# Token rows for the experts: turned by VectorE instead of TensorE, from the third pass on

## The chip, the cores and the metric

One core of one Trainium2 chip runs the whole program. The metric is the device time of one launch in microseconds, median of the runs; lower is better. All numbers are float32.

## The reference, cut to what matters

The model runs 512 tokens of 1024 features through two layers of a first block and then one layer of a second block. The change touches only the mixture of experts, which each of the two layers of the first block has. There each token picks one of 4 groups of experts and in it 2 of 8 experts, so 1024 pairs of token and expert are spread over 32 experts:

```python
g_sel = jnp.argmax(g_logits, axis=-1)
top_p, top_i = lax.top_k(e_prob, TOP_K)          # TOP_K = 2, in the token's group
expert_id = (g_sel[:, None] * EXPERTS_PER_GROUP + top_i).reshape(-1)
...
hid = jax.nn.silu(xb @ w_gate[e]) * (xb @ w_up[e])   # xb: the expert's tokens, 1024 features
return hid @ w_down[e]                               # hidden width 256
...
ys = ys * slot_gate[:, None].astype(ys.dtype)
out = jax.ops.segment_sum(ys, slot_tok, num_segments=N + 1)[:N]
```

## The kernel before

Only the expert part matters here; it runs once in layer 0 (about 484 to 775 us of the profiled execution) and once in layer 1 (about 1328 to 1618 us). Its work is cut into NSEQ = 24 passes. 16 of them are "main" passes: each takes two experts, 64 lanes (slots for tokens) for each, 128 lanes in all. 8 are "tail" passes for the tokens beyond 64 of an expert. The order is written out: main, tail, main, main, tail, main, and so on, so that each three passes in a row hold two main passes and one tail pass.

**Weights.** A main pass needs 6 units of 1 MB: 4 for gate and up (`experts_gu`), 2 for down (`experts_down`). SP loads them in the order of use into `ring`, which has 6 places. A load is issued when the place's last user, a group of matmuls on TensorE, is done (`load`, L3185; function `experts`). A tail pass takes its weights from `TW`, filled by indirect DMAs from GpSimd (POOL), L3053 and L3062, for rows that exist; where no expert has such tokens the indices lie out of bounds and nothing but tiny descriptors move.

**Token rows.** The normalised tokens lie in DRAM as `h_tokens` (512 rows of 4 KB). For pass q POOL gathers 128 rows by one indirect DMA (`gather`, L3032) into `XG[:, q % 2]`, with a table of row numbers `idx` that VectorE has made from counts; empty lanes are out of bounds. The matmuls need features on partitions, so TensorE turns the rows: `turn_x` (L1011) makes 8 transposes of 128x128 against the identity into PSUM, ScalarE copies them to `XGT[:, q % 2]` (`x_copy`, L2777), and `gate_up` (L1037) reads them as the stationary operand.

**The rest of a pass.** `gate_up(q)`: 32 matmuls into one bank; ScalarE's silu (`gate`, L2783); VectorE's product (`hidden`, L1986); two transposes on TensorE (`turn_hidden`, L1047), copied by VectorE (`turned_hidden`, L1979); `down(q)`: 16 matmuls (L1059); VectorE scales the result by the gates (`rows`, L1997); POOL scatters the rows to `expert_rows` in DRAM (`scatter`, L3039).

**Order.** Each engine's order is written out by hand, with semaphores between them. TensorE in the steady state: `turn_hidden(q-1)`, `turn_x(q+1)`, `gate_up(q)`, `down(q-1)`. VectorE: `turned_hidden(q)`, `hidden(q+1)`, `rows(q)`. POOL: `gather(q+2)`, then the tail's weights where one is due, then `scatter(q-2)`. In layer 1 VectorE and ScalarE also work out two tables of sines and cosines (`trig`, lines from L1562 on and L2847 on) after the passes 8 and 14 of this order. Indirect DMAs go by the queue q0 (software_dynamic), the ring's loads by q1 (hardware_dynamic); both are served by the same 16 DMA engines.

The lines that set a pass's two ends on TensorE and the loads behind it:

```python
pe.wait_ge(w_landed[place], 16 * fill)            # unit(): a unit of weights has landed
...
name, value = used[(place, fill - 1)]             # load(): its place is free again
sp.wait_ge(Q[name], value)
```

## Time and profile before

| | us |
|---|---|
| median of 3 runs | 3021.24 |
| lowest and highest | 3016.02, 3024.18 |
| span of the profiled execution | 3017.0 |
| of it: expert part of layer 0, first transpose to last `down` | 486.8 to 772.6 |
| of it: expert part of layer 1 | 1328.4 to 1617.8 |

The profile is of one execution. Its own time is not reported apart from the span of 3017.0 us, which lies inside the range of the runs and 4.2 us under their median. The page gives each engine's busy time and, in 40 slices, the busy share of the 16 DMA engines. PE is TensorE's matmuls, DVE is VectorE, ACT is ScalarE, POOL is GpSimd, SP issues loads. The expert parts are the slices in which the DMA digit is 9.

### The profile page before, as it was taken

How to read it: one execution, taken by the hardware profiler on the slowest of the kernel's cores; microseconds unless marked ns; L12 is line 12 of the kernel's file. 1: busy time of each engine (PE TensorE's matmuls, PEld its weight loads, DVE VectorE, ACT ScalarE, POOL GpSimd, SP SyncE). 2: the span in 40 equal slices, each digit the busy share in tenths (PEclk: the TensorE clock that was granted, in tenths of full speed). 3: DMA queues.
4: the chain of work that ended last, by engine and by line, in shares of the span. 5: the costliest groups of instructions: out<-in, count | busy, mean ns of one | idle time of the engine just before them, and what ended most of it. 6: DMA issues, size and time to landing. Idle time of an engine off the chain costs nothing.

```text
span 3017.0 us, 31787 instructions
## 1 busy us (share of the span) xinstructions
PE 2943.6 (98%) x12506; PEld 1884.5 (62%) x12506; DVE 1308.3 (43%) x2213; ACT 652.7 (22%) x1083; POOL 820.3 (27%) x625
## 2 busy tenths in 40 slices
PE   9999999999899999999998999999999999999998
PEld 7865464333468754643333688888664445888887
DVE  6733443111546435431225644433563464644442
ACT  2035313111210253231112300002112441300011
POOL 5400022222135000222222145542300102254442
PEclk9999999999999999999999999999999999999999
DMA  5211125999522101249996122222211201222220
GB/s 190 84 70 43 54 79 225 388 387 384 205 84 84 70 29 56 85 171 387 379 377 274 70 84 92 90 93 89 86 75 56 84 29 56 80 88 84 84 98 28
DMA packets 81379, 412.67 MB, mean 137 GB/s; under 512 B 25872, under 2 KB 26256, under 8 KB 34768
## 3 DMA queue, kind: packets, MB, share of 16 engines
q1 hardware_dynamic: 56608, 387.57, 33.7%
q0 software_dynamic: 24624, 23.08, 2.3%
q8 instruction: 99, 1.62, 0.2%
q14 instruction: 48, 0.39, 0.0%
HBM read 513.31 MB, written 31.46 MB: 181 GB/s over the span
## 4 chain that ended last, share of the span: by engine, by line
PE 67%; DVE 5%; ACT 1%; issue 1%; DMA 0%; DVEq 0%; POOL 0%; ACTq 0%
PE PS L1103 33%; PE PS L608 6%; PE PS L1037 5%; PE PS L1276 3%; PE PS L569 3%; PE PS L594 3%; PE PS L1059 3%; PE PS L686 2%; PE PS L840 1%; PE PS L895 1%; PE PS L516 1%; PE PS L1339 1%; PE PS L1011 1%; PE PS L1319 1%; PE PS L781 1%
## 5 line engine op out<-in xcount | busy, mean ns | idle before, releaser
L3086 POOL TENSOR_TENSOR ATT<-ring 128x512 f32<-128x512 f32 (+1 forms) x98 | 128.0, 1306 | 1203.4 <-PE PS L1103 689.8
L1103 PE MATMUL PS<-G,ATT 128*128 128x256 f32 x1360 | 321.6, 379 | 0.0
L1103 PE MATMUL PS<-HT,ring 128*128 128x256 f32 x1392 | 317.8, 379 | 3.8 <-ACT HT L2626 2.1
L1103 PE MATMUL PS<-G,ring 128*128 128x256 f32 x1232 | 291.4, 379 | 0.0
L1103 PEld LDWEIGHTS PS<-HT,ring 128*128 128x128 f32 x1392 | 264.1, 190 | 43.6 <-issue 3.5
L1103 PEld LDWEIGHTS PS<-G,ATT 128*128 128x128 f32 x1360 | 258.4, 190 | 36.4 <-issue 0.9
L608 PE MATMUL PS<-HT,ring 128*128 128x512 f32 x576 | 263.2, 600 | 0.0
L2808 ACT ACTIVATE TMP<-PS 128x256 f32<-128x256 f32 x92 | 35.2, 383 | 1053.2 <-PE PS L1103 935.9
L1103 PEld LDWEIGHTS PS<-G,ring 128*128 128x128 f32 x1232 | 234.1, 190 | 31.8
L1037 PE MATMUL PS<-ring,G 128*64 128x512 f32 x1024 | 226.8, 595 | 0.6 <-ACT G L2777 0.6
L608 PEld LDWEIGHTS PS<-HT,ring 128*128 128x128 f32 x576 | 104.5, 190 | 126.6 <-issue 120.2
L3094 POOL TENSOR_TENSOR ATT<-ring 128x512 f32<-128x512 f32 (+1 forms) x97 | 172.2, 1776 | 7.6
L1986 DVE TENSOR_TENSOR G<-PS,G 128x256 f32<-128x256 f32 x48 | 20.4, 425 | 319.4 <-ACT G L2783 319.1
L2057 DVE TENSOR_TENSOR BIG<-PS,TMP 128x256 f32<-128x256 f32 x100 | 42.4, 424 | 258.2 <-ACT TMP L2808 255.3
L1037 PEld LDWEIGHTS PS<-ring,G 128*64 128x64 f32 x1024 | 70.7, 137 | 134.0 <-issue 133.0
L1103 PE MATMUL PS<-HT,ATT 128*128 128x256 f32 x568 | 134.3, 379 | 0.0
L3088 POOL TENSOR_TENSOR ATT<-ring 128x512 f32<-128x512 f32 (+1 forms) x97 | 130.5, 1345 | 0.0
L3039 POOL DMA_INDIRECT expert_rows<-G,ATT x46 | 46.6, 1012 | 308.4 <-DVE G L1997 307.9
L3091 POOL TENSOR_TENSOR ring<-ATT,ring 128x512 f32<-128x512 f32 (+1 forms) x98 | 127.8, 1304 | 7.7
L1059 PE MATMUL PS<-ring,G 128*64 128x512 f32 x512 | 116.1, 594 | 9.7 <-DVE G L1979 5.9
L2057 DVE TENSOR_TENSOR G<-PS,TMP 128x256 f32<-128x256 f32 x40 | 17.0, 424 | 245.3 <-ACT TMP L2808 242.5
L2057 DVE TENSOR_TENSOR TMP<-PS,TMP 128x256 f32<-128x256 f32 x273 | 115.8, 424 | 10.6 <-PE PS L1103 1.3
(383 smaller groups left out, 4370.0 us busy)
## 6 DMA issues: line engine op xcount, KB each, us to landing
ring<-in_stream SPq DMA_DIRECT2D x163, 1024.0 KB
ring<-in_experts_gu SPq DMA_DIRECT2D x128, 1024.0 KB
ring<-in_experts_down SPq DMA_DIRECT2D x64, 1024.0 KB
G<-expert_rows SPq DMA_DIRECT2D x8, 1024.0 KB, 7.6
h_tokens<-G POOLq DMA_DIRECT2D x2, 2048.0 KB, 7.6
XT<-in_xT SPq DMA_DIRECT2D x1, 1024.0 KB, 8.4
G<-in_pT POOLq DMA_DIRECT2D x2, 512.0 KB, 6.2
out_T<-XT SPq DMA_DIRECT2D x2, 512.0 KB, 3.7
```

Of the source, the lines that this page charges most:

```text
L569: mm = pe.matmul(ps[0:m, :], wv[:, k, c:c + m], rhs[:, k, :], start=k == 0, stop=k == nk - 1)
L594: mm = pe.matmul(ps, w[:, k, c:c + P], rhs[:, k, :], start=k == 0, stop=k == nk - 1)
L608: mm = pe.matmul(units["ps"], w[:, k, c:c + P], rhs[:, k, :], start=k == 0, stop=k == KD - 1)
L1037: mm = pe.matmul(PS[r, 4 + q % 2, :], XGT[:, q % 2, k * P + CAP * side:k * P + CAP * (side + 1)], ws[side][:, kk * 512:(kk + 1) * 512], st ...
L1059: mm = pe.matmul(PS[r, n, :], HIDT[:, q % 2, j * P + CAP * side:j * P + CAP * (side + 1)], ws[side][:, j * D + n * 512:j * D + (n + 1) * 512],
L1103: mm = pe.matmul(product(g, name), x[:, k * P:(k + 1) * P], y[:, k, :], start=first and k == 0 and name in opening, stop=last and k == h - ...
L1276: mm = pe.matmul(ps, w[:, k, m % 2 * P:(m % 2 + 1) * P], HP[:, k, :], start=k == 0, stop=k == KD - 1)
L2057: v.tensor_tensor(out, product(g, x), y, ALU.add).then_inc(Q[name], now.inc(name))
L3086: pool.tensor_tensor(a["S1"], a["A21"], a["A22"], ALU.add)\
L3088: pool.tensor_tensor(a["S3"], a["A11"], a["A21"], ALU.subtract)\
L3091: pool.tensor_tensor(a["S2"], a["S1"], a["A11"], ALU.subtract)\
L3094: pool.tensor_tensor(a["S4"], a["A12"], a["S2"], ALU.subtract)\
```

## The change

From the third pass on (q = 2 to 23, 22 passes in each layer) `turn_x` and `x_copy` are gone. POOL gathers a pass's rows by four indirect DMAs of 128 pieces of 1 KB (`gather_squares`). Piece g brings, for the 32 lanes of block g, the i-th quarter of each row to the 32 partitions of block i, so that one VectorE instruction, which transposes each 32x32 block in place on the partitions (`turned_rows`), puts features on partitions. Feature f then lies on partition f // 8, block f % 8, so the host lays out the rows of the gate and up weights in the same interleaved order; the first two passes keep TensorE's transposes, with a stride of 8. The row numbers of the pieces come from four small matmuls (`quad_tables`) behind the first `gate_up`, and VectorE turns them into a table (`quad_rows`). The order of the other work is kept. The core of the diff:

```diff
@@ -37,6 +37,9 @@
...
 PLE = 256
+SQUARE = 32
+SQUARES = P // SQUARE
+QD = D // SQUARES
@@ -208,6 +211,7 @@
...
     moe[:, 208] = i
+    moe[:, 209] = i // SQUARE
     moe[:, 216:216 + NSEQ] = P * np.arange(NSEQ)[None, :]
@@ -261,6 +265,7 @@
...
         HDR = nc.dram_tensor("h_tokens", (S, D), F32, kind="Internal").ap()
+        HQR = HDR.rearrange("t (i d) -> (t i) d", i=SQUARES)
         YDR = nc.dram_tensor("expert_rows", (2 * S, D), F32, kind="Internal").ap()
@@ -329,7 +334,7 @@
...
                        ("lanes", 2 * TT * P), ("pairs", 2 * TT * 3 * NSEQ), ("tab", 2 * NSEQ), ("idx", 2 * NSEQ),
-                       ("gslot", NSEQ)):
+                       ("gslot", NSEQ), ("quad", SQUARES * NSEQ)):
             RT[_n] = ATT[:, _o:_o + _w]
@@ -351,6 +356,7 @@
...
         LAST_TOKENS = RT["lanes"][:, 0:S]
+        QUAD_LANES = RT["lanes"][:, S:2 * S]
         RX = BIG[:, 0:KD, :]
@@ -359,6 +365,10 @@
...
         HTF = HT[:, :, :].rearrange("p a b -> p (a b)")
+
+        def gathered(L, q):
+
+            return 16 * (L * (1 + SQUARES * (NSEQ // 2 - 1)) + 1 + SQUARES * (q // 2))
@@ -1003,13 +1013,10 @@
...
                     g = f"x_gather{q % 2}"
-                    if q > 1:
-                        pe.wait_ge(Q["x_copied"], at[f"moe{L}"]["x_copied"] + q)
-                    pe.wait_ge(Q[g], now.next(g, 16))
+                    pe.wait_ge(Q[g], gathered(L, q))
                     o = turned_at(q)
                     for k in range(KD):
-                        mm = pe.transpose(PSF[:, o + k * P:o + (k + 1) * P],
-                                          XG[:, q % 2, k * P:(k + 1) * P], IDENT)
+                        mm = pe.transpose(PSF[:, o + k * P:o + (k + 1) * P], XG[:, q % 2, k:D:KD], IDENT)
                     mm.then_inc(Q["x_turned"], now.inc("x_turned"))
@@ -1026,8 +1033,17 @@
...
+                def quad_tables():
+
+                    pe.wait_ge(Q["tab_ready"], now.next("tab_ready"))
+                    for g in range(SQUARES):
+                        mm = pe.matmul(PS[:, 7, g * NSEQ:(g + 1) * NSEQ], QUAD_LANES[:, g * P:(g + 1) * P], RT["tab"][:, 0:NSEQ],
+                                       start=g == 0, stop=True, skip_group_check=True)
+                    mm.then_inc(Q["quads_ready"], now.inc("quads_ready"))
+
                 def gate_up(q):
-                    pe.wait_ge(Q["x_copied"], now.next("x_copied"))
+                    name = "x_copied" if q < 2 else "x_blocks"
+                    pe.wait_ge(Q[name], now.next(name))
                     for half in range(2):
@@ -1064,19 +1080,17 @@
...
-                at[f"moe{L}"] = {"x_turned": now.count("x_turned"), "x_copied": now.count("x_copied")}
+                at[f"moe{L}"] = {"x_turned": now.count("x_turned"), "x_blocks": now.count("x_blocks")}
                 at[f"moe{L}_y"] = now.count("y_ready")
...
                 gate_up(0)
+                quad_tables()
                 gate_up(1)
                 turn_hidden(0)
-                turn_x(2)
                 down(0)
...
                     turn_hidden(q - 1)
-                    if q + 1 < NSEQ:
-                        turn_x(q + 1)
                     gate_up(q)
@@ -1966,6 +1980,11 @@
...
                 v.tensor_copy(r["gslot"], PS[:, 7, 2 * NSEQ:3 * NSEQ]).then_inc(Q["dve_step"], now.inc("dve_step"))
+                v.wait_ge(*now.prev())
+                v.tensor_copy(QUAD_LANES.rearrange("p (g i x) -> p g i x", g=SQUARES, i=SQUARES),
+                              IDENT.rearrange("p (g x) -> p g x", g=SQUARES).unsqueeze(2)
+                              .to_broadcast([P, SQUARES, SQUARES, SQUARE]))\
+                    .then_inc(Q["tab_ready"], now.inc("tab_ready"))
@@ -1977,6 +1996,22 @@
...
                     v.tensor_copy(HIDT[:, q % 2, :], PS[:, 6, 0:256]).then_inc(Q["hidT_ready"], now.inc("hidT_ready"))
+
+                def quad_rows():
+
+                    v.wait_ge(Q["quads_ready"], now.next("quads_ready"))
+                    v.wait_ge(*now.prev())
+                    v.tensor_scalar(r["quad"].bitcast(I32), PS[:, 7, 0:SQUARES * NSEQ], float(SQUARES), MC[:, 209:210],
+                                    ALU.mult, ALU.add)\
+                        .then_inc(Q["quad_rows"], now.inc("quad_rows"))
+
+                def turned_rows(q):
+
+                    v.wait_ge(Q[f"x_gather{q % 2}"], gathered(L, q))
+                    v.wait_ge(*now.prev())
+                    v.transpose(XGT[:, q % 2, :].rearrange("p (j g x) -> p g j x", j=KD, g=SQUARES),
+                                XG[:, q % 2, :].rearrange("p (g x j) -> p g j x", j=KD, g=SQUARES))\
+                        .then_inc(Q["x_blocks"], now.inc("x_blocks"))
@@ -1998,8 +2033,11 @@
...
                 hidden(0)
+                quad_rows()
                 for q in range(NSEQ):
                     turned_hidden(q)
+                    if q + 2 < NSEQ:
+                        turned_rows(q + 2)
                     if q + 1 < NSEQ:
@@ -2788,8 +2826,6 @@
...
                     gate(q)
-                    if q + 2 < NSEQ:
-                        x_copy(q + 2)
                     if L == LAYERS - 1 and q == TRIG_AT[0] + 1:
@@ -3019,7 +3055,7 @@
...
-            idx, widx = RT["idx"].bitcast(U32), RT["widx"].bitcast(U32)
+            idx, quad, widx = (RT[n].bitcast(U32) for n in ("idx", "quad", "widx"))
             IOA = bass.IndirectOffsetOnAxis
@@ -3032,6 +3068,16 @@
...
                                         oob_is_err=False).then_inc(Q[f"x_gather{q % 2}"], 16)
+
+            def gather_squares(q):
+
+                c = column(q)
+                for g in range(SQUARES):
+                    i = g * NSEQ + c
+                    pool.indirect_dma_start(out=XG[:, q % 2, g * QD:(g + 1) * QD], out_offset=None, in_=HQR,
+                                            in_offset=IOA(ap=quad[:, i:i + 1], axis=0),
+                                            bounds_check=SQUARES * S - 1,
+                                            oob_is_err=False).then_inc(Q[f"x_gather{q % 2}"], 16)
@@ -3125,11 +3171,16 @@
...
                 no_rows()
-                x0, y0 = at[f"moe{L}"]["x_turned"], at[f"moe{L}_y"]
+                x0, b0, y0 = at[f"moe{L}"]["x_turned"], at[f"moe{L}"]["x_blocks"], at[f"moe{L}_y"]
                 for q in range(NSEQ + 1):
                     if q + 2 < NSEQ:
-                        pool.wait_ge(Q["x_turned"], x0 + q + 1)
-                        gather(q + 2)
+                        if q == 0:
+                            pool.wait_ge(Q["quad_rows"], now.next("quad_rows"))
+                        if q < 2:
+                            pool.wait_ge(Q["x_turned"], x0 + q + 1)
+                        else:
+                            pool.wait_ge(Q["x_blocks"], b0 + q - 1)
+                        gather_squares(q + 2)
                     if 1 <= q < NSEQ and ORDER[q - 1][0] == "tail" and ORDER[q - 1][1] + 1 < TAILS:
@@ -3272,7 +3323,8 @@
...
     out["stream"] = np.stack(stream + f1 + mix + f2)
-    gu = np.concatenate([a[n].reshape(LAYERS, NE, KD, P, EH) for n in ("w_exp_gate", "w_exp_up")], axis=4)
+    gu = np.concatenate([a[n].reshape(LAYERS, NE, P, KD, EH) for n in ("w_exp_gate", "w_exp_up")], axis=4)
+    gu = gu.transpose(0, 1, 3, 2, 4)
     gu = gu.reshape(LAYERS, NE, 2, KD // 2, P, 2 * EH).transpose(0, 1, 4, 2, 3, 5).reshape(LAYERS, NE, P, 2, UNIT)
```

How the instructions stand, at three places. First TensorE at the start of the expert part of layer 0, before (L1011 is `turn_x`, L1037 `gate_up`, L1047 `turn_hidden`, L1059 `down`):

```order
245 L1011 MATMUL PS<-MATS,G 128x128 x16
246 L1037 MATMUL PS<-ring,G 64x512 x16
247 L1037 MATMUL PS<-BIG,G 64x512 x16
248 L1047 MATMUL PS<-MATS,G 128x128 x2
249 L1011 MATMUL PS<-MATS,G 128x128 x8
250 L1059 MATMUL PS<-ring,G 64x512 x8
251 L1047 MATMUL PS<-MATS,G 128x128 x2
252 L1011 MATMUL PS<-MATS,G 128x128 x8
253 L1037 MATMUL PS<-ring,G 64x512 x16
```

and now (L1019 is `turn_x`, L1053 `gate_up`, L1040 `quad_tables`, L1063 `turn_hidden`, L1075 `down`):

```order
245 L1019 MATMUL PS<-MATS,G 128x128 x16
246 L1053 MATMUL PS<-ring,G 64x512 x16
247 L1040 MATMUL PS<-ATT 128x24 x4
248 L1053 MATMUL PS<-BIG,G 64x512 x16
249 L1063 MATMUL PS<-MATS,G 128x128 x2
250 L1075 MATMUL PS<-ring,G 64x512 x8
251 L1063 MATMUL PS<-MATS,G 128x128 x2
252 L1053 MATMUL PS<-ring,G 64x512 x16
```

The groups of 8 transposes that stood before each `down` and each `gate_up` are gone, and 4 small matmuls stand between the first two `gate_up`.

VectorE at the same place, now (L2021 is `hidden`, L2004 `quad_rows`, L1998 `turned_hidden`, L2012 `turned_rows`, L2032 `rows`):

```order
429 L2021 TENSOR_TENSOR G<-PS,G 128x256
430 L2004 TENSOR_SCALAR ATT<-PS,MC 128x96
431 L1998 COPY G<-PS 128x256
432 L2012 STREAM_TRANSPOSE G<-G 128x4x8x32
433 L2021 TENSOR_TENSOR G<-PS,G 128x256
434 L2032 TENSOR_SCALAR G<-PS,ATT 128x1024
435 L1998 COPY G<-PS 128x256
436 L2012 STREAM_TRANSPOSE G<-G 128x4x8x32
```

The transpose of pass q+2 stands between the copy of the turned hidden rows of pass q and the product `hidden` of pass q+1.

POOL's queue, now (L3068 is `gather`, L3077 `gather_squares`, L3085 `scatter`, L3099 and L3108 the tail's weights):

```order
71 L3077 DMA G<-h_tokens,ATT 128x256 x12
72 L3099 DMA BIG<-in_experts_gu,ATT 128x4096 x2
73 L3085 DMA expert_rows<-G,ATT 1024x1024
74 L3077 DMA G<-h_tokens,ATT 128x256 x4
75 L3085 DMA expert_rows<-G,ATT 1024x1024
76 L3108 DMA BIG<-in_experts_down,ATT 128x2048 x2
```

Where one gather of 128x1024 stood for a pass, four of 128x256 stand now; the scatters and the tail's loads queue behind them in the old order.

## Rows read from the trace of the kernel before

**Rows 1.** The page: the span, each engine's busy time, the DMA share in 40 slices.

```profile
span 3017.0 us, 31787 instructions
...
PE 2943.6 (98%) x12506; PEld 1884.5 (62%) x12506; DVE 1308.3 (43%) x2213; ACT 652.7 (22%) x1083; POOL 820.3 (27%) x625
...
DMA  5211125999522101249996122222211201222220
```

**Rows 2.** Timeline of PE, layer 0, two passes and a late one: start, length, line, count [idle before].

```profile
567.61 7.09 PE L1037 MATMUL PS<-BIG,G 128*64 128x512 f32 x32
...
578.06 0.44 PE L1047 MATMUL PS<-MATS,G 128*128 128x128 f32 x2
578.33 1.04 PE L1011 MATMUL PS<-MATS,G 128*128 128x128 f32 x8
579.30 7.09 PE L1037 MATMUL PS<-ring,G 128*64 128x512 f32 x32
...
598.61 3.65 PE L1059 MATMUL PS<-ring,G 128*64 128x512 f32 x16 [0.53 <-issue]
```

**Rows 3.** Waits of PE in the expert part of layer 0 (484 to 775 us): total, times, longest.

```profile
PE PS L1059 <- DVE G L1979: 1.7, 1, 1.7
PE PS L1059 <- issue: 1.6, 4, 0.5
```

**Rows 4.** Busy time of the engines, granted clock, DMA share and GB/s, 490 to 770 us.

```profile
490.00:770.00 280.00, 276.63 (x1364) 104.17 (x1362) 49.91 (x71) 33.09 (x48) 74.53 (x75) 1.00 0.93 367
```

**Rows 5.** DMA queues in the same stretch: packets, MB, share of 16 engines.

```profile
q1 hardware_dynamic: 12971, 94.38, 83.6%
q0 software_dynamic: 11011, 8.14, 9.2%
```

**Rows 6.** SP's loads of the ring of weights, 577 to 599 us: start, length, count.

```profile
578.17 6.01 SPq L3185 DMA_DIRECT2D ring<-in_experts_gu  x4
586.43 9.06 SPq L3185 DMA_DIRECT2D ring<-in_experts_down  x4
```

**Rows 7.** Groups of VectorE instructions that read and write 1024 elements in SBUF.

```profile
L2133 DVE TENSOR_TENSOR BIG<-BIG,ATT 128x1024 f32<-128x1024 f32 x22 | 45.4, 2064 | 2.3
...
L1544 DVE STREAM_SHUFFLE G<-BIG 128x1024 f32<-128x1024 f32 x12 | 15.9, 1326 | 0.0
```

**Rows 8.** Timeline of POOL, 517 to 536 us.

```profile
521.61 1.01 POOL L3039 DMA_INDIRECT expert_rows<-G,ATT  x1 [9.35 <-DVE G L1997]
...
524.24 1.00 POOL L3062 DMA_INDIRECT BIG<-in_experts_down,ATT  x1 [0.30 <-issue]
```

**Rows 9.** DMA queues, 540 to 541.5 us.

```profile
q1 hardware_dynamic: 88, 0.62, 99.2%
q0 software_dynamic: 87, 0.00, 3.3%
```

**Rows 10.** DMA queues, 522 to 525 us.

```profile
q1 hardware_dynamic: 174, 1.28, 100.8%
```

**Rows 11.** DMA queues, 542.5 to 544 us.

```profile
q1 hardware_dynamic: 25, 0.11, 17.3%
q0 software_dynamic: 298, 0.00, 10.2%
```

**Rows 12.** DMA queues, 512 to 522 us, with the count of small packets.

```profile
DMA packets 917, 4.06 MB, mean 406 GB/s; under 512 B 360, under 2 KB 360, under 8 KB 484
...
q0 software_dynamic: 424, 0.51, 14.2%
```

**Rows 13.** Timeline of VectorE at the first passes, layer 0.

```profile
496.61 0.42 DVE L1986 TENSOR_TENSOR G<-PS,G 128x256 f32<-128x256 f32 x1 [12.91 <-ACT G L2783]
503.36 0.42 DVE L1979 COPY G<-PS 128x256 f32<-128x256 f32 x1 [6.33 <-PE PS L1047]
```

**Rows 14.** Timeline of PE at the third pass, layer 0.

```profile
508.95 3.22 PE L1037 MATMUL PS<-ring,G 128*64 128x512 f32 x14
```

**Rows 15.** Timeline of PE behind the first angle block, layer 1.

```profile
1454.09 3.65 PE L1059 MATMUL PS<-ring,G 128*64 128x512 f32 x16 [1.23 <-DVE G L1979]
```

More of the change, by code:

```diff
@@ L275, in build_program @@
                  "gate_scaled rf_ready sum2_ready x1_sum late_sum rtok_sum rtok_ready xp_ready pool_step unit_done wsum_ready t_ready hidden_ready m1_ready silu_done tile_done toep_landed "
-                 "pl_landed gain_landed x_low x_high x_landed pos_landed pos2_landed lam_exp tails_zeroed rx_zeroed hot_ready hot_taken z_store part_done edge_sq edge_tile xsq_ready xsq_used res_scaled res_sum x_0 x_1 w_0 w_1 w_2 gates_scaled roped").split()
+                 "pl_landed gain_landed x_low x_high x_landed pos_landed pos2_landed lam_exp tails_zeroed rx_zeroed tab_ready quads_ready quad_rows x_blocks hot_ready hot_taken z_store part_done edge_sq edge_tile xsq_ready xsq_used res_scaled res_sum x_0 x_1 w_0 w_1 w_2 gates_scaled roped").split()
         Q = {n: ctx.enter_context(nc.semaphore(n)) for n in names}
```

## The prediction

> **What bounds the kernel now.** I began with the page [rows 1]: TensorE is busy 98% of 3017.0 us, and the DMA digit is 9 in the two expert parts alone. Then the timeline of TensorE [rows 2]: a pass takes 579.30 - 567.61 = 11.69 us with no gap, and `turn_x` holds TensorE for 579.30 - 578.33 = 0.97 us of it. Read alone, that says the whole of `turn_x` can be had: 22 passes x 2 layers x 0.97 = 42.7 us. The waits speak against it [rows 3]: `down` waited four times, 1.6 us in all, for something that is no engine, that is, for its weights. Over 280 us the DMA engines are busy 93% [rows 4], with 83.6% for the ring of weights and 9.2% for the indirect DMAs [rows 5]. So TensorE and the weights are nearly level, and what matters is where in three passes the weights are late.
>
> Three passes use 12 units, in 6 places. After the second main pass's `down` (over at 578.06) SP issues four loads for gate and up and two for `down` [rows 6]; TensorE wants the last two at 598.61 - 0.53 = 598.08, and starts at 598.61 [rows 2]. These six loads filled 20.55 us, and TensorE's own work in that stretch is 20.02 us. Two of the cycle's three `turn_x` lie in the stretch. Without them TensorE would be there 1.94 us sooner and wait for weights that come no sooner. Only the third `turn_x`, behind that `down`, shortens the cycle.
>
> **What is removed.** 22 x 8 transposes and 22 copies on ScalarE per layer. From q = 4 on these are 7 cycles of three passes, less one pass: 7 x 0.97 = 6.8 us per layer gained, 13.6 in both. ScalarE's copies lay beside matmuls and count nothing. The bounds of this term: nothing, and 20.5 us in a layer, if the weights could follow.
>
> **VectorE's transposes**, 22 per layer. No such instruction is in the trace. The nearest row is STREAM_SHUFFLE of 128x1024, which also moves data between partitions: 1.33 us; the dearest plain group of this size is 2.06 us [rows 7]. I take 1.33, with 1.2 to 2.7 as bounds (2.7, twice the shuffle, for a source read with a stride of 8). The instruction stands between `turned_hidden(q)` and `hidden(q+1)`, which wait for a `gate_up` of 6.9 us in between. VectorE is busy 49.91 of 280 us [rows 4]. That hides it in all passes but the first. If the cover goes (the rows land late), it and all of `hidden` behind it stand in TensorE's path.
>
> A rule of the Trainium skill speaks against it: "SBUF — State Buffer", in the note on cachelines of 16 bytes, says that accesses which cross to a new line each time pay a penalty. Each element of this source, 32 bytes apart, does; by it the instruction would be nearer to the upper bound. No row here shows it.
>
> **The gathers.** Four DMA_INDIRECT for one. On POOL each has a pitch of 1.31 us (521.61 to 524.24 for two) [rows 8], so a pass costs POOL 3.9 us more. Its 75 instructions of the stretch [rows 4] become 141, x 1.31 = 185 of 280 us: hidden.
>
> On the DMA engines an indirect DMA is 11011 / 75, about 147 packets, 9 per engine [rows 4, 5]. Where both queues are full they are served one for one: 88 packets of the ring, 87 of q0 in 1.5 us, that is 0.27 us per turn on each engine [rows 9]. The ring alone makes 174 in 3 us [rows 10], the same rate, so empty lanes cost the ring nothing; without a ring q0 runs freely, 298 in 1.5 us [rows 11]. Rows that exist cost bytes: in 10 us 124 packets of 4 KB and 300 small ones took 14.2% of 160 us = 22.7 us; with 9 ns for a small one (3.3% of 24 us / 87 [rows 9]) a row takes (22.7 - 2.7) / 124 = 161 ns [rows 12]. A piece of 1 KB I estimate at 161 / 4 + 9 = 49 ns, so four cost 35 ns more than a row. Some 950 rows of a layer x 35 / 16 engines = 2.1 us, two thirds in the stretch that the loads fill: +1.4 us per layer. The upper bound counts the 6650 further small ones too, x 9 / 16 = 3.7 us, of which 2.5: +3.9 in all; the lower is 0.
>
> The Trainium skill, "DMA: Bandwidth & Descriptors", section on queues, rings and completion order, says that an engine changes queues only after a whole packet of some 9 to 17 descriptors. By that a gather's 9 would go in one turn, and four gathers in four. The trace shows single descriptors taking turns, 88 to 87, with the weights' rate undisturbed; a block of 9 per load would give the same ratio, so this one is not closed, and it is a rival below.
>
> **The start.** The row numbers wait for four matmuls behind `gate_up(0)`: at 8 transposes in 1.04 us [rows 2], 0.5 us. `quad_rows` follows `hidden(0)`, done at 497.03 [rows 13], so the four gathers of pass 2 start at 497.3, the last at 501.2. With the ring full nothing of q0 is served for 3.4 us or more (issued 521.61, none before 525 [rows 8, 10]); with 9 turns of 0.27 and a landing of about 1 it lands near 508.5. VectorE holds `hidden(1)` until then: + 1.33 + 0.42, and `gate_up(2)` begins near 510.6, where before it began at 508.95 [rows 14]. +1.6 us per layer; bounds -1.4 (TensorE decides) and +4.5 (3 us later).
>
> **The angle blocks.** In layer 1 TensorE waited 1.23 us for VectorE behind the first of the two [rows 15]. It comes 0.97 us sooner now and waits as much longer: +1.9 in all; bounds 0 and +5 (if the new transpose falls in it).
>
> **Sum.** Per layer -6.8 + 1.4 + 1.6 = -3.8; two layers -7.6; with the angle blocks -5.7 us. The profiled execution has a span of 3017.0, which becomes 3011.3. It is 4.2 us under the median, and I take the difference over: 3021.24 - 5.7 = 3015.5 us. About 0.3%, 9 us, is what a measurement of this kernel can tell from no change, so this counts as the same.
>
> **Rivals.**
>
> *A. The weights can follow.* For: `down` is late in four of eight cycles only, by 0.5 us at most [rows 3], and 7% of the DMA time is free [rows 4]. Against: the gap lies where no place of the ring is free. The floor is 0.93 x 280 = 260 us, + 3 for pieces, against 280: -17 us per layer at the most, about 2989 with the angle blocks; half of it gives 3004. It decides if the loads of the stretch of 20.55 us end 1 us or more before their use.
>
> *B. The rows come late (slower).* Three passes have 3 scatters, 4 loads for tails and 3 gathers on q0: 10 DMAs, 90 turns per engine, beside 12 loads x 9 = 108 of the ring. Now they are 19 DMAs, 171 turns: 63 more than the ring can pair. They must go in the ring's gap of about 2 us per cycle [rows 11], else q0 is backlogged. The loop for one buffer: transpose 1.3 + four issues 5.2 + a scatter and tail loads on POOL 3.9 + start 3.4 + up to 63 turns x 0.27 = 17 + landing 1 = 32 us, against two passes and what TensorE can still do, 21.5 + 6.9 + 1.6 = 30. From a backlog of some 55 turns on, VectorE waits in each cycle, `hidden` behind it, then TensorE. At 1.5 to 3 us per cycle, 7 cycles and 2 layers: +21 to +42, less the 5.7: 3036 to 3057. The margin is thin, but in a wait the ring stands still and q0 empties at once [rows 11], which holds the price to the lower half: 3036.
>
> *C. The transpose is dear* (2.7 us or more). It costs 1.4 more at the start of each layer and up to 3 in the angle blocks: 3021. It cannot be seen against no change.
>
> *D. Whole gathers take one turn.* The even count [rows 9] allows it too. Pass 2 then lands about 2 us sooner in both layers, and nothing is ever backlogged: 3015.5 - 4 = 3011.5. It is the rule of the Trainium skill, "DMA: Bandwidth & Descriptors", cited above.
>
> **How the numbers follow.** Forecast 0.42, A 0.15, B 0.27, C 0.08, D 0.08. Faster by over 0.3% (under 3012.2): all of A but a little, most of D, a fifth of the forecast: 0.28. Slower by over 0.3% (over 3030.3): B, and a little of the forecast's upper bounds: 0.28. Within: 0.44. The range leaves out the low half of A and the upper end of B: 3000 to 3040. The forecast's own range is 3008 to 3024.
>
> **What the profile would show.** Right: TensorE's passes of 10.7 us where no `down` waits; `down` of the first main pass of a cycle late by about 2 us in each cycle, put to no engine; a cycle of 34 to 34.5 us; about 20500 packets on q0 in the stretch; VectorE's transpose near 1.3 us, mostly with no wait. It is wrong by B if VectorE's transpose waits on the DMA in many passes and `turn_hidden` waits for `hidden`; wrong by A if no `down` is late and a cycle is near 33 us.

## The result, and the profile after

The changed kernel takes 3029.91 us (median of 9 runs, 3026.83 to 3033.59); the kernel before, on the same chip, 3019.98 (9 runs, 3015.08 to 3024.18). The ratio is 1.0034, with a 95% interval of 1.0025 to 1.0043: about 10 us slower. The profiled execution has a span of 3029.5 us against 3017.0. The forecast was 3015.5 us, a small gain, in a range of 3000 to 3040. The prediction held that changes under 0.3% can't be told from none; the interval here is 0.2% wide, so the loss is told clearly.

The page of the changed kernel, beside [rows 1]: the span, the busy time of the engines.

```profile
span 3029.5 us, 31343 instructions
PE 2919.5 (96%) x12170; PEld 1851.6 (61%) x12170; DVE 1397.8 (46%) x2261; ACT 608.1 (20%) x1039; POOL 955.4 (32%) x757
```

The stretch of [rows 4] and its DMA queues, as in [rows 5]: busy PE, PEld, DVE, ACT and POOL with their counts, granted clock, DMA share, GB/s; then packets, MB, share.

```profile
490.00:770.00 280.00, 258.22 (x1174) 85.98 (x1172) 93.02 (x91) 9.42 (x24) 141.04 (x140) 0.99 0.94 366
q1 hardware_dynamic: 12971, 94.44, 84.8%
q0 software_dynamic: 11973, 7.80, 9.0%
```

VectorE's new instruction, the group of layer 0, beside [rows 7]:

```profile
L2012 DVE STREAM_TRANSPOSE G<-G 128x1024 f32<-128x1024 f32 x22 | 44.9, 2042 | 3.9 <-DMA G<-h_tokens,ATT 1.4 <-DVE G L1998 0.5
```

TensorE is 276.63 - 258.22 = 18.4 us less busy over 280 us, as intended. POOL issued 140 indirect DMAs instead of 75, yet q0's packets rose only from 11011 to 11973. VectorE's transpose takes 2.04 us and waited 3.9 us in 22 passes for its rows.

The timeline of TensorE from the third pass on, layer 0, beside [rows 14]: start, length, line, count [idle before <- releaser].

```profile
509.86 7.09 PE L1053 MATMUL PS<-ring,G 128*64 128x512 f32 x32
516.78 4.09 PE L1075 MATMUL PS<-BIG,G 128*64 128x512 f32 x16
526.96 0.69 PE L1063 MATMUL PS<-MATS,G 128*128 128x128 f32 x2 [6.09 <-DVE G L2021]
527.58 9.14 PE L1053 MATMUL PS<-ring,G 128*64 128x512 f32 x32
```

What no step of the prediction had: a pause of 6.09 us, once in the layer. TensorE waited for VectorE's `hidden`, and that for ScalarE's `gate`. ScalarE's row names no engine that it waited for ("remote"):

```profile
504.67 0.38 ACT L2821 ACTIVATE G<-PS 128x256 f32<-128x256 f32 x1 [7.64 <-PE PS L1053]
526.00 0.39 ACT L2821 ACTIVATE G<-PS 128x256 f32<-128x256 f32 x1 [20.95 <-remote]
```

It needs only `gate_up(2)`, whose matmuls end by the records at 509.86 + 7.09 = 516.95. It starts at 526.00, 9 us later. SP's next loads, which TensorE's completions release too, start at the same moment:

```profile
526.00 8.14 SPq L3236 DMA_DIRECT2D ring<-in_experts_down  x4
```

Here and below, "completions" are the semaphore events with which TensorE tells the other engines that a group of matmuls is done. After the idle time the granted clock is down (0.50 in the row below), and `gate_up(3)` takes 9.14 instead of 7.09 us:

```profile
525.00:530.00 5.00, 3.04 (x8) 1.06 (x10) 3.21 (x4) 0.39 (x1) 0.91 (x1) 0.50 1.01 389
```

Layer 1 has it at the same pass, and there the matmuls of `down(1)` themselves stand apart:

```profile
1362.85 1.89 PE L1075 MATMUL PS<-BIG,G 128*64 128x512 f32 x8
1364.98 1.02 PE L1075 MATMUL PS<-BIG,G 128*64 128x512 f32 x3 [0.24 <-issue]
1366.41 2.02 PE L1075 MATMUL PS<-BIG,G 128*64 128x512 f32 x4 [0.41 <-issue]
1369.25 0.59 PE L1075 MATMUL PS<-BIG,G 128*64 128x512 f32 x1 [0.82 <-issue]
1373.17 0.69 PE L1063 MATMUL PS<-MATS,G 128*128 128x128 f32 x2 [3.33 <-DVE G L2021]
```

A late completion that no engine's row explains sends one to the engines that were busy without a break just then. POOL's timeline of layer 0:

```profile
498.76 1.05 POOL L3077 DMA_INDIRECT G<-h_tokens,ATT  x1 [6.85 <-DVE ATT L2004]
...
509.65 1.00 POOL L3077 DMA_INDIRECT G<-h_tokens,ATT  x1 [0.69 <-issue]
...
522.77 1.00 POOL L3077 DMA_INDIRECT G<-h_tokens,ATT  x1 [0.30 <-issue]
529.09 1.02 POOL L3085 DMA_INDIRECT expert_rows<-G,ATT  x1 [5.32 <-DVE G L2032]
```

From 498.76 to 523.77 it issues 19 indirect DMAs at a pitch of 1.31 us, with one gap of 0.69. `gate` starts 2.2 us after the last. VectorE's copy behind `turn_hidden(1)`, at the ninth DMA of the run, is late too: it starts at 511.69, 1.8 us after the matmuls' end by the records (509.93) and 0.9 us after VectorE was free for it.

**Where the time went.** The expert part of a layer falls into pieces by TensorE's timeline: the start (first `turn_x` to the end of `down(0)`); eight stretches, each from the end of a second main pass's `down` (the first: of `down(0)`) to the start of the next `down` of a first main pass, with six ring loads in it; and seven rests, each from the start of that `down` to the end of the next, where the third `turn_x` of the cycle stood. The eighth stretch has no loads to wait for; with the last `down` it is 12.94 + 3.65 us everywhere, and it is in the last column alone. Sums in us, layer 0 / layer 1, one profiled execution each:

| kernel | start | first stretch | stretches 2 to 7 | rests | layer |
|---|---|---|---|---|---|
| before | 21.0 / 21.1 | 19.9 / 19.8 | 121.0 / 121.8 | 107.3 / 110.1 | 285.8 / 289.4 |
| changed | 22.0 / 22.1 | 27.3 / 27.4 | 125.2 / 123.8 | 101.2 / 107.4 | 292.3 / 297.3 |
| one_gather | 22.0 / 22.1 | 20.4 / 20.0 | 122.4 / 121.8 | 101.3 / 107.4 | 282.7 / 287.8 |
| before_pieces | 23.3 / 23.4 | 20.3 / 20.0 | 123.7 / 124.5 | 107.4 / 110.2 | 291.2 / 294.6 |
| empty_run | 25.7 / 24.6 | 19.8 / 19.8 | 121.6 / 122.2 | 107.3 / 110.1 | 291.0 / 293.2 |
| third_only | 21.0 / 21.1 | 20.6 / 20.6 | 123.0 / 123.7 | 101.2 / 107.4 | 282.4 / 289.4 |
| stretch_only | 21.0 / 21.1 | 20.6 / 20.6 | 119.7 / 120.0 | 107.4 / 110.2 | 285.3 / 288.5 |

The changed kernel gained 6.1 us in the rests of layer 0 (2.8 in layer 1), lost 4.2 and 2.1 in the stretches, 1.0 at the start, and 7.4 and 7.6 in the first stretch, which holds the pause. Outside these parts the same instructions take up to 4 us more or less from one execution to the next (between the two expert parts 552.7 to 556.8 us), so a few microseconds of a whole run are not read from one timeline.

### The profile page after: what moved, and what is told of

Read it like the earlier page. It is cut to its first block, busy times and chain, and to the rows that moved or that the text cites. A ratio compares the mean times of both kernels' runs of the same rounds, so it can differ in the third digit from the quotient of the medians.

```text
span 3029.5 us, 31343 instructions
## 1 busy us (share of the span) xinstructions
PE 2919.5 (96%) x12170; PEld 1851.6 (61%) x12170; DVE 1397.8 (46%) x2261; ACT 608.1 (20%) x1039; POOL 955.4 (32%) x757
## 4 chain that ended last, share of the span: by engine, by line
PE 87%; DVE 5%; DMA 4%; another core or an unknown queue 1%; ACT 1%; issue 1%; SPq 0%; POOL 0%; DVEq 0%; ACTq 0%; POOLq 0%
PE PS L1117 37%; PE PS L1053 8%; PE PS L618 8%; PE PS L604 5%; PE PS L1075 4%; PE PS L696 4%; PE PS L579 4%; PE PS L1290 4%; DMA ring<-in_experts_gu 3%; PE PS L850 1%; PE PS L791 1%; PE PS L538 1%; PE PS L905 1%; PE PS L914 1%
## 5 line engine op out<-in xcount | busy, mean ns | idle before, releaser
L2844 ACT ACTIVATE TMP<-PS 128x256 f32<-128x256 f32 x92 | 35.3, 384 | 1056.9 <-PE PS L1117 939.7
L1053 PE MATMUL PS<-ring,G 128*64 128x512 f32 x1024 | 233.3, 605 | 10.4 <-DMA ring<-in_experts_gu 9.9
L3077 POOL DMA_INDIRECT G<-h_tokens,ATT x176 | 177.5, 1009 | 110.9 <-issue 49.3
L1053 PEld LDWEIGHTS PS<-ring,G 128*64 128x64 f32 x1024 | 73.0, 139 | 148.2 <-issue 147.4
L1075 PE MATMUL PS<-ring,G 128*64 128x512 f32 x512 | 117.9, 602 | 27.2 <-issue 19.7
L2821 ACT ACTIVATE G<-PS 128x256 f32<-128x256 f32 x48 | 18.4, 384 | 520.3 <-PE PS L1053 329.4
L2021 DVE TENSOR_TENSOR G<-PS,G 128x256 f32<-128x256 f32 x48 | 20.4, 425 | 222.0 <-ACT G L2821 156.8
```

The source lines that it names most:

```text
L1053: mm = pe.matmul(PS[r, 4 + q % 2, :], XGT[:, q % 2, k * P + CAP * side:k * P + CAP * (side + 1)], ws[side][:, kk * 512:(kk + 1) * 512], st ...
L1075: mm = pe.matmul(PS[r, n, :], HIDT[:, q % 2, j * P + CAP * side:j * P + CAP * (side + 1)], ws[side][:, j * D + n * 512:j * D + (n + 1) * 512],
L3077: pool.indirect_dma_start(out=XG[:, q % 2, g * QD:(g + 1) * QD], out_offset=None, in_=HQR, in_offset=IOA(ap=quad[:, i:i + 1], axis=0), bou ...
```

## The experiments

Theory 1 was that POOL's run of gathers makes the pause; theory 2, that it belongs to TensorE's or VectorE's changed program. Each ratio is to the kernel before, run beside it on the same chip. Of each edit its core is shown; in a diff "..." marks what is left out.

**one_gather**: the piece gathers undone alone (with the counts that the engines wait for).

```diff
-                        gather_squares(q + 2)
+                        gather(q + 2)
```

> From the third pass on, the rows are gathered whole again (one indirect DMA per pass instead of four); VectorE's 32x32 transposes, the row-number matmuls and TensorE's shorter program stay. The rows then stand in the wrong order for the transposes, so the output of the expert part isn't the reference's. Theory 1 (the pause of about 8.5 us of TensorE once per layer, at the third pass, comes from POOL's run of 12 back-to-back piece gathers): the pause is gone in both layers, -17, and the pieces' bytes (about -2 in each layer) too: 3009 to 3013 us. Theory 2 (the pause belongs to TensorE's or VectorE's changed program, whatever POOL does): the pause stays, 3024 to 3028 us.

Measured: 3011.93 us, ratio 0.9972 (0.9960 to 0.9983). No pause: TensorE's changed program and VectorE's transposes don't make it by themselves. The third pass, where the changed kernel waits:

```profile
516.83 3.60 PE L1075 MATMUL PS<-BIG,G 128*64 128x512 f32 x16
520.37 0.44 PE L1063 MATMUL PS<-MATS,G 128*128 128x128 f32 x2
520.73 7.32 PE L1053 MATMUL PS<-ring,G 128*64 128x512 f32 x32
```

The stretches 2 to 7 are 2.8 and 2.0 us shorter than in the changed kernel: the price of the pieces in the flow.

**from_sixth**: passes 2 to 5 keep the old way, on every engine (`FIRST = 6`).

```diff
-                        gather_squares(q + 2)
+                        (gather if q + 2 < FIRST else gather_squares)(q + 2)
...
```

> The change begins at the seventh pass (q = 6) instead of the third: passes 2 to 5 use the old way (one gather, TensorE's turn, ScalarE's copy). Theory 1 (burst of gathers behind the late row numbers makes the pause): no burst at the start of the layer, POOL has caught up by then, so no pause; 3029.9 - 17 + 4 passes whose turn_x is back, of which one or two count (2 to 4 us over both layers): 3014 to 3018 us. Theory 2 (the pause comes at the first passes with the new way, wherever they stand): it moves to passes 6 and 7, 3029 to 3033 us.

Measured: 3019.20 us, 0.9991 (0.9982 to 1.0001). No pause in either layer, at pass 6 neither. The sum for the rest was too hopeful by 1 to 5 us.

**before_pieces**: the kernel before, its gathers from the third pass on in four pieces.

```diff
-                        gather(q + 2)
+                        gather_pieces(q + 2)
```

> The kernel before with one edit: from the third pass on the rows are gathered in four pieces of 1 KB, into the same places, so the result is the same; TensorE still turns them. Theory 1: the burst of piece gathers costs here too, a pause at the third pass or a start later by several us per layer: 3030 us or more. Theory 2: pieces cost their bytes alone, 0 to 4 us per layer: 3021 to 3028, no pause. My prediction's term of 1.4 us per layer would give 3023.

Measured: 3026.31 us, 1.0021 (1.0011 to 1.0030). The pieces alone lose 2.3 and 2.2 us at the start of the layers, and 3.0 and 2.9 in the stretches. The pause is there, one pass earlier, as POOL's run is (482 to 501 us). TensorE's first row and ScalarE's `gate(0)`:

```profile
488.29 7.09 PE L1040 MATMUL PS<-ring,G 128*64 128x512 f32 x32 [0.24 <-ACT G L2784]
...
503.51 0.38 ACT L2790 ACTIVATE G<-PS 128x256 f32<-128x256 f32 x1 [14.15 <-remote]
```

The gate comes 503.51 - 495.38 = 8.1 us late, once more 2 us after POOL's last issue.

**early_rows**: the row numbers from VectorE, ahead of the expert part.

```diff
-                quad_tables()
...
+                    v.tensor_scalar(r["quad"][:, g * NSEQ:(g + 1) * NSEQ].bitcast(I32), r["tab"][:, 0:NSEQ], float(SQUARES),
+                                    float(g), ALU.mult, ALU.add).then_inc(Q["quad_rows"], now.inc("quad_rows"))
```

> The changed kernel with the pieces' row numbers worked out by VectorE from the slot table before the expert part (as 4 x row + g), so the four matmuls behind the first gate_up and the wait for them are gone and pass 2's gathers are issued at about 492 instead of 499 us. Each piece then goes to a lane where it does not belong, so the output of the expert part isn't the reference's; the traffic is the same. If the pause comes from POOL's backlog behind late row numbers, it is gone or under 3 us: 3012 to 3018. If it comes from the pieces or the transposes themselves, it stays: 3026 to 3030.

Measured: 3022.04 us, 1.0006 (0.9996 to 1.0017), between the two guesses. The run starts earlier and is shorter (15 DMAs), and `gate(0)` is 7.7 and 7.3 us late; most of it lies beside `gate_up(1)`, so the start takes 22.7 and 22.4 us, 1.8 and 1.3 more than before. In layer 1 the stretches 2 to 7 take 128.9 us, 5 more than in the changed kernel; no row here says why.

**paced**: POOL waits until the pass's gather before has landed, for the passes 3 and 4.

```diff
+                        if q in (1, 2):
+                            pool.wait_ge(Q[f"x_gather{(q + 1) % 2}"], gathered(L, q + 1))
                         gather_squares(q + 2)
```

> The changed kernel with one edit on POOL: the piece gathers of the fourth and fifth pass (q = 3 and 4) wait for the landing of the gather before them, so that at most four gathers are issued in a row at the start of a layer. If an unbroken run of 8 or more indirect DMAs on POOL is what holds TensorE's completions back (theory 1, after the first four runs), the pause at the third pass is gone or under 2 us: 3012 to 3016 us. If it comes from the rows' bytes, the transposes or the place in the program, it stays: 3027 to 3031.

Measured: 3031.76 us, 1.0037 (1.0022 to 1.0051); the expectation failed, and told more than a hit. Two groups of four pass with little harm, and the third pass has no pause. Then POOL makes up what it lost, 23 DMAs from 518.73 to 548.8 us, and TensorE is disturbed from 532 to 550:

```profile
535.04 8.57 PE L1053 MATMUL PS<-BIG,G 128*64 128x512 f32 x32 [3.12 <-issue]
543.42 1.41 PE L1075 MATMUL PS<-ring,G 128*64 128x512 f32 x4
545.63 0.63 PE L1075 MATMUL PS<-ring,G 128*64 128x512 f32 x1 [0.80 <-issue]
```

**empty_run**: in the kernel before, behind the gather of pass 3 (`EMPTY_RUN = 8`):

```diff
...
+                for i in range(EMPTY_RUN):
+                    pool.indirect_dma_start(out=RT["dump"][:, 16 * i:16 * (i + 1)], out_offset=None, in_=small,
+                                            in_offset=IOA(ap=idx[:, column(2):column(2) + 1], axis=0),
+                                            bounds_check=0, oob_is_err=False).then_inc(Q["dumped"], 16)
```

> The kernel before, with 8 more indirect DMAs on POOL behind the gather of the fourth pass (from about 494.2 to 504.8 us), each a gather of 64-byte rows in which all lanes but at most one are out of bounds; the data go to a scratch tile. Nothing waits for them but POOL's own queue. Theory 1a (issuing alone holds TensorE's completion signals back): TensorE pauses in pass 1 or 2 by 2 to 8 us per layer, 3025 to 3035 us. Theory 1b (it takes rows with bytes, 1 KB pieces, in the run): no pause, 3019 to 3022 us.

Measured: 3028.10 us, 1.0031 (1.0018 to 1.0044): 9 us for 16 DMAs that move next to nothing. TensorE's `turn_x(2)`, which waits for nothing of theirs, then POOL's first and last DMA of the run:

```profile
503.66 0.86 PE L1012 MATMUL PS<-MATS,G 128*128 128x128 f32 x5
504.91 0.33 PE L1012 MATMUL PS<-MATS,G 128*128 128x128 f32 x1 [0.38 <-issue]
505.61 0.32 PE L1012 MATMUL PS<-MATS,G 128*128 128x128 f32 x1 [0.37 <-issue]
506.99 0.27 PE L1012 MATMUL PS<-MATS,G 128*128 128x128 f32 x1 [1.07 <-issue]
...
482.96 1.07 POOL L3033 DMA_INDIRECT G<-h_tokens,ATT  x1 [10.70 <-DVE ATT L1963]
...
503.93 1.00 POOL L3055 DMA_INDIRECT ATT<-h_tokens,ATT  x1 [0.30 <-issue]
```

But the empty DMAs do less than the full ones. `gate_up(0)` ends at 496.59, at the eleventh DMA of the run, and its `gate` is 2.0 us late, not 8.1 as in before_pieces at the eleventh; and it starts in the midst of the run, not behind it:

```profile
498.59 0.38 ACT L2784 ACTIVATE G<-PS 128x256 f32<-128x256 f32 x1 [8.03 <-remote]
```

The copy behind `turn_hidden(0)`, at the sixteenth, is 3.4 us late (507.26, where the matmuls end at 503.82).

**spaced_run**: empty_run with a memset of 0.79 us ahead of each of the 8.

```diff
                 for i in range(EMPTY_RUN):
...
+                    pool.memset(RT["filled"], 0.0).then_inc(Q["filled"], now.inc("filled"))
```

> The kernel before with the 8 empty gathers, each behind a memset of 128x800 (about 0.7 us), so that the issues have a pitch of about 2.1 instead of 1.31 us. If issues back to back are what holds TensorE (a queue that fills faster than it empties), the pause is gone: 3018 to 3022 us. If the number of indirect DMAs counts, or POOL's being without a wait, it stays: 3026 to 3032 us.

Measured: 3019.70 us, 1.0001 (0.9991 to 1.0011). The same 8 DMAs at a pitch of 1.95 us cost nothing, though POOL is without a break for longer (`gate(0)` is still 0.8 us late, hidden beside `gate_up(1)`):

```profile
503.27 1.04 PE L1012 MATMUL PS<-MATS,G 128*128 128x128 f32 x8
504.24 3.65 PE L1060 MATMUL PS<-ring,G 128*64 128x512 f32 x16
...
503.05 1.00 POOL L3058 DMA_INDIRECT ATT<-h_tokens,ATT  x1 [0.16 <-issue]
504.06 0.78 POOL L3057 MEMSET ATT<- 128x800 f32 x1
505.00 1.00 POOL L3058 DMA_INDIRECT ATT<-h_tokens,ATT  x1 [0.16 <-issue]
```

**empty_four**: `EMPTY_RUN = 4`.

> As the kernel before with the empty gathers, but 4 of them instead of 8: POOL's unbroken run from 483 us ends near 500 instead of 505 us. If TensorE's completions are held from about the tenth DMA of an unbroken run until the run ends, the hold is about 5 us shorter, and mostly hidden: pass 2 starts at most 1 us later than in the kernel before, 3019 to 3023 us. If each empty gather costs a fixed sum, half of the 9 us: 3023 to 3025.

Measured: 3019.19 us, 1.0004 (0.9994 to 1.0014); the start is 21.0 us as before. `gate(0)` is 2.0 and 2.2 us late here too, but that lies beside `gate_up(1)`, and the run is over before TensorE needs an answer. Not a price per DMA.

**busy_run**: the loop holds only a memset of 128x900, ten times (9.0 us).

> The kernel before with 10 memsets of 128x900 on POOL in place of the empty gathers, about the same 10 us of unbroken work at the same place, no DMA. If any busy POOL holds TensorE's completions, a pause like that of the empty gathers, 3025 to 3030 us. If it is the issuing of indirect DMAs, nothing: 3018 to 3021 us.

Measured: 3020.28 us, 0.9997 (0.9988 to 1.0007). No `gate` is later than before. A busy POOL as such does no harm.

**spaced_pieces**: back in the changed kernel.

```diff
                 for g in range(SQUARES):
                     i = g * NSEQ + c
+                    if 3 <= q <= 4:
+                        if now.count("filled"):
+                            pool.wait_ge(Q["filled"], now.count("filled"))
+                        pool.memset(RT["filled"], 0.0).then_inc(Q["filled"], now.inc("filled"))
```

> The changed kernel with a memset of 128x700 (0.7 us) on POOL ahead of each piece gather of the fourth and fifth pass, so that these 8 issues have a pitch of about 1.9 instead of 1.31 us. Nothing else moves, and the result is the reference's. If back-to-back issues make the pause, it is gone or under 2 us at the third pass, 3013 to 3018 us; it may return at passes 5 to 7, where POOL makes up the lost time back to back, then 3022 to 3030. If something else of the change makes it, it stays at the third pass, 3030 us.

Measured: 3020.97 us, 0.9995 (0.9985 to 1.0004): 9 us under the change's median (0.39% by the two ratios), by doing more. The third pass:

```profile
517.10 3.60 PE L1075 MATMUL PS<-BIG,G 128*64 128x512 f32 x16
520.63 0.44 PE L1063 MATMUL PS<-MATS,G 128*128 128x128 f32 x2
521.00 7.09 PE L1053 MATMUL PS<-ring,G 128*64 128x512 f32 x32
```

A smaller one stays behind it: `gate(3)` is 3.0 us late, and `gate_up(4)` takes 8.41 us. What else lengthens its layers (289.0 and 292.0 us in the profiled execution) is TensorE's clock, which falls behind two waits for weights in each:

```profile
566.00 5.25 PE L1075 MATMUL PS<-ring,G 128*64 128x512 f32 x16 [2.46 <-issue]
```

The same `down` takes 3.65 us at the full clock; here the granted clock is 0.59 from 566 to 570 us.

**gaps_all**: one memset per group of four, from the fourth pass on.

```diff
+                        if q >= 1:
...
+                            pool.memset(RT["filled"], 0.0).then_inc(Q["filled"], now.inc("filled"))
                         gather_squares(q + 2)
```

> The changed kernel with one memset of 128x700 (0.7 us) on POOL ahead of each pass's four piece gathers, from the fourth pass on; the four are still back to back. If a short gap every 4 to 7 DMAs is enough to break the run, no pause: 3012 to 3016 us. If the mean pitch counts (1.31 becomes about 1.45 us), the pause is only shorter: 3020 to 3028 us.

Measured: 3028.72 us, 1.0026 (1.0015 to 1.0038). The pause moves to the fourth and fifth pass. `gate(3)` is 8.1 and 8.6 us late; in the change `gate(2)` was 9.1 and 9.2. A gap per group is not enough. Over what length of a run the pitch has to be wider isn't tested.

**third_only** (`NEW = range(5, 24, 3)`) and **stretch_only** (`NEW = [q for q in range(6, 24) if q % 3 != 2]`): the new way for the passes in `NEW` alone.

```diff
-                        gather_squares(q + 2)
+                        (gather_squares if q + 2 in NEW else gather)(q + 2)
```

> The new way only for the passes q = 5, 8, ... 23, whose turn_x stands behind the down of the first main pass, outside the stretch that six ring loads fill; all others in the old way, and the row-number matmuls behind turn_hidden(1). The result is the reference's. If my reading of the cycle is right, all of the gain is here: 7 x -0.86 = -6.0 and pieces for 7 of 22 passes, +1, so -5 per layer and about 3010 us, with no pause. If the gain is spread over all passes (or TensorE's work bounds everywhere), a third of it: 3016 or more.

> The opposite choice: the new way only for the passes q >= 6 whose turn_x lies in the stretch of the six ring loads (12 passes per layer), q = 5, 8, ... 23 in the old way. By my reading of the cycle the 12 x 0.97 = 11.6 us per layer that TensorE is spared there are given back whole as waits for weights, and the pieces of 12 passes cost 1 to 2 us: 3021 to 3024 us. If the weights can follow (rival A), it is faster by up to 20 us: 3000 to 3010.

Measured: third_only 3011.96 us, 0.9972 (0.9961 to 0.9984); stretch_only 3017.17 us, 0.9992 (0.9983 to 1.0002). Seven passes per layer give 7 us by the medians; the twelve others, with more of TensorE's time removed, nothing that can be told from none. The profiled execution of third_only shows only half of the 7: 3.4 us in layer 0 and none in layer 1, where the gain of the rests (2.8) goes again in the first stretch (0.8, with the row-number matmuls in it) and in the stretches 2 to 7 (2.0). Where the other half lies isn't shown. In stretch_only the stretches 2 to 7 are 1.3 and 1.8 us shorter, of 11.6 us removed. The rest of the spared time stands as waits for weights at the end of a stretch:

```profile
590.07 3.65 PE L1060 MATMUL PS<-ring,G 128*64 128x512 f32 x16
594.31 3.65 PE L1060 MATMUL PS<-ring,G 128*64 128x512 f32 x16 [0.59 <-DMA ring<-in_experts_gu]
599.29 3.65 PE L1082 MATMUL PS<-ring,G 128*64 128x512 f32 x16 [1.33 <-issue]
```

third_only computes the reference's result and is the fastest of those here that do: 7 us under the kernel before, 18 under the change.

**turned_twice**: one_gather with each transpose done twice (`for name in ("dve_step", "x_blocks")` around it).

> The kernel with whole gathers (one_gather, 3011.9 us), with each of VectorE's transposes done twice, so that it costs 4.1 instead of 2.05 us; the output of the expert part isn't the reference's, as there. If VectorE's turn is covered by gate_up in all passes but those of the start and the angle blocks, as the prediction says, it adds 2 us per layer at the start and up to 2 in each angle block: 3012 to 3020 us. If it is on the path in every pass, 2.05 x 22 x 2 = 90 us more.

Measured: 3013.71 us, 0.9979 (0.9970 to 0.9989), 1.8 us over one_gather, which ran on another chip. By the timeline its first stretch is 1.8 and 1.9 us longer, and of the rest only one angle block moved (the rests of layer 1 are 1.7 us shorter): the transpose is on the path once per layer, and else covered. Those 1.7 us are not the transpose's: they are the clock behind the wait of that block (see "The angle blocks" below).

## Why the prediction was wrong, point by point

**The step that failed** is the one on POOL: "Its 75 instructions of the stretch [rows 4] become 141, x 1.31 = 185 of 280 us: hidden." The count was right (140), and so was the share. The step put the price of issuing at nothing because POOL had time left, and left out where these instructions stand. At the start of a layer the row numbers come late, the gathers of passes 2, 3 and 4 and all that waits behind them on POOL go out back to back, 19 in a row, and such a run holds TensorE's completions (9 us late at its fourteenth DMA). That costs 6.9 and 7.5 us in the first stretch (27.3 against 20.4, 27.4 against 20.0 in one_gather), 14.3 us in all. Shown by: no pause with one gather per pass, nor with the old way in the first passes; a pause in the kernel before from pieces alone, and from gathers without rows; none from the same gathers spaced out, nor from memsets; and none at the third pass of the changed kernel once the pieces are spaced. What is not shown is the way in the chip. One rival within it is untested: a wider pitch thins out both POOL's issuing and the descriptors that it puts on q0, so no run says which of the two holds the completions. The DMA engines were not full meanwhile: from 517 to 524 us q0 takes 18.2% of their time and the ring 36.5%.

**The gathers' bytes** (+1.4 us per layer, bounds 0 to 3.9) were undersized: 2.8 and 2.0 by one_gather, 3.0 and 2.9 by before_pieces. That its bounds hold these is luck, for the mechanism was another. The term took a piece of 1 KB for a packet of its own, so that q0 would need more of the DMA engines' time. From 480 us to just behind layer 0's last `down` (774 us before, 779 in before_pieces) q0 has 11520 packets before and 12576 in before_pieces: 1056 more, which is 16 for each of the 66 further DMAs, and only 20 packets have 512 B to 2 KB. So the pieces went several to a packet, and q0's own time hardly rose. It is the ring's packets that took longer, the same 13125. Before (294 us), then before_pieces (299 us), packets, MB, share:

```profile
q1 hardware_dynamic: 13125, 95.60, 81.0%
q0 software_dynamic: 11520, 8.43, 9.1%
...
q1 hardware_dynamic: 13125, 95.60, 80.8%
q0 software_dynamic: 12576, 8.45, 9.1%
```

That is 238.1 and 241.6 us for the ring, 26.8 and 27.2 for q0. Why the ring's packets took longer isn't shown.

**What is removed** (-6.8 us per layer, the third `turn_x` only). The rests fell by 6.1 in layer 0, 0.87 each instead of 0.97; and that the other two `turn_x` of a cycle give little is what stretch_only shows: 1.3 and 1.8 us of 11.6, with the price of its pieces already taken off. But the stretches were not as fixed as I had them: with whole gathers they grew by 0.5 + 1.3 us in layer 0 and 0.2 in layer 1, though no load was added to them. The ring has less idle time when the rest is shorter: the DMA share is 0.93 in one_gather too [rows 4], so the loads are nearly the bound of the whole cycle. That this is why is my reading; no run tests it alone.

**The start** (+1.6 us per layer): 1.0, the four matmuls for the row numbers (1.07 us, where I had 0.5). The gathers of pass 2 landed in time.

**VectorE's transpose** (1.33 us taken, bounds 1.2 to 2.7): 2.04 us, as much as the dearest plain group of [rows 7]. It hid behind `gate_up` as forecast. The price is in the direction of the rule of the Trainium skill ("SBUF — State Buffer", cachelines of 16 bytes), but no run here reads a source without a stride, so the rule is not tested.

**The angle blocks** (+1.9 us): +3.3, by how much longer the rests of layer 1 are than those of layer 0 (107.36 - 101.24 = 6.1 us, and 110.11 - 107.31 = 2.8 before). The wait grew nearly as foreseen, from 1.23 [rows 15] to 2.04 us; what I had not counted is that TensorE's clock can fall after it:

```profile
1466.43 5.35 PE L1075 MATMUL PS<-ring,G 128*64 128x512 f32 x16 [2.04 <-DVE G L1998]
...
1468.00:1472.00 4.00, 4.00 (x14) 1.27 (x10) 0.91 (x3) 0.00 (x0) 2.32 (x3) 0.70 0.10 39
```

The same `down` takes 3.65 us in [rows 15]. The granted clock of the second row, 0.70, is a mean of four microseconds between 1.2 and 2.4 GHz. It is not sure to fall: at this same place, behind a wait of 2.03 or 2.04 us, `down` takes 5.35 us in the changed kernel, one_gather, third_only and gaps_all, but 3.65 in from_sixth, early_rows, paced, spaced_pieces and turned_twice. So 1.7 of the 3.3 us look like luck of the execution; no kernel was profiled twice to show it.

Put together, without the pause (the first stretch taken from one_gather) the layers come to -0.3 and +0.4 us, where I had -3.8 and -1.9: no gain. spaced_pieces, which has next to no pause at the third pass, measures the same by its median.

**The rivals.** A (the weights can follow) is refuted by stretch_only, which had 1.3 and 1.8 us of 11.6. B (the rows come late) had the sign and nearly the size, 3036 us, but not the mechanism: q0 carried 11973 packets, not some 20500, and VectorE waited 3.9 us in 22 passes for its rows. The price came with POOL's run of DMAs, not from rows that land late. That the measured time lies in the range of 3000 to 3040 us is owed to B's price, and so is luck. C (a dear transpose): 2.04 us more of it cost 1.8 and 1.9 us in the first stretch of turned_twice, near the 1.4 per layer that C had for 1.4 us. D: q0's packets per DMA fell from 147 to 86, fewer than there are lanes. That points the way of the rule of the Trainium skill ("DMA: Bandwidth & Descriptors", several descriptors to a packet); it gained no time here.

**The signs.** Passes of 10.8 us with no gap, and a `down` of the first main pass that is late in each cycle and put to no engine, came as forecast: a cycle of the changed kernel in TensorE's timeline, from the second main pass's `down` to the next late one. The `down` is late by 1.0 to 1.9 us in layer 0, not by 2. The cycle of 34 to 34.5 us did not come: it is 14.47 + 20.87 = 35.3 in the mean of layer 0, before 35.5.

```profile
583.12 3.60 PE L1075 MATMUL PS<-ring,G 128*64 128x512 f32 x16
...
593.94 3.60 PE L1075 MATMUL PS<-BIG,G 128*64 128x512 f32 x16
...
607.28 3.65 PE L1075 MATMUL PS<-ring,G 128*64 128x512 f32 x16 [1.37 <-issue]
```

## What to carry to other kernels

Cost an added instruction not by its engine's share but by the longest unbroken run that it makes, above all where several passes' work is released at once. Where two resources are nearly level, change only the places where the slower one isn't waited for: seven of 22 passes gave here as much (3011.96 us) as all 22 with whole gathers (3011.93). And when a completion is late that its own engine's rows don't explain, look which engine was busy without a gap, and test it with the same instructions moving nothing, then with the same instructions spaced.

## What the runs showed of the hardware

- Indirect DMAs issued by GpSimd back to back at a pitch of 1.31 us delay TensorE's completions from about the ninth of a run on. With pieces of 1 KB in the run the delay is 1.7 us or so at the ninth and 7 to 10 us from the eleventh on, and the completion comes some 2 us after the run's last issue in the change, before_pieces and early_rows (19 in a run: 6.9 and 7.5 us of the layer lost; 15: 2.3). Empty ones delay too, but less: 2.0 us at the eleventh, with the run still going on, 3.4 at the sixteenth (17 in a run: 3.4 and 4.8 us lost). At a pitch of 1.9 us the delay is 0.8 us and costs nothing; with a memset of 0.7 us every four to seven of them it is still 8 us. Whether TensorE's matmuls run slowly then or only its completion signals are late can't be told from the records: in one place the matmuls' records run on and ScalarE starts 8 to 9 us later, in others single matmuls stand 0.4 to 1.1 us apart. Why it happens in the chip stays open.
- A 32x32 block transpose of 128x1024 on VectorE, source with a stride of 8 elements, takes 2.04 us.
- Four gathers of 128 pieces of 1 KB for one of 128 rows of 4 KB made only 9% more packets on their queue (11973 against 11011), 16 for each further DMA, and took the ring's packets 3.5 us more of the DMA engines' time in a layer.
- Behind a wait of TensorE of 2.03 or 2.04 us at one and the same place its next group of 16 matmuls took 5.35 us in four kernels and 3.65 in five.
